# Encoder block, one core: the opening's loads asked for in another order, and the first scale part in two halves

## The reference, cut to what matters

```
mod = silu(c) @ w_ada + b_ada                      # 6 x 2048 columns: shift1, scale1, gate1, shift2, ...
h   = rmsnorm(x, g_mix) * (1 + scale1) + shift1
z   = h @ w_in                                     # latents (832 columns), GQA q, k, v, two branch gates
...                                                # two attentions, output projection, expert-choice FFN
```

## Time and profile before

| | |
|---|---|
| time, median of 3 runs | 2217.11 us (2216.94 to 2217.76) |
| the profiled execution | 2216.92 us, span 2214.6 us, mean granted TensorE clock 0.991 |
| TensorE busy (PE) | 2124.1 us, 96% of the span |
| VectorE busy (DVE) | 871.9 us, 39% |
| ScalarE busy (ACT) | 566.4 us, 26% |
| chain of work that ended last | TensorE 84%, DMA 8%, VectorE 4%, ScalarE 1% |
| DMA | 635.61 MB, 287 GB/s over the span |

### The profile page before, as it was taken

How to read it: one execution, slowest core, us unless ns; L and a number is a source line. 1 busy time by engine, 2 the same in 40 slices (tenths; PEclk the granted TensorE clock), 3 DMA queues, 4 the chain that set the end, 5 groups by cost and what they waited for, 6 DMA issues and landing times.

```text
span 2214.6 us, 26365 instructions
## 1 busy us (share of the span) xinstructions
PE 2124.1 (96%) x10338; PEld 1380.8 (62%) x10338; DVE 871.9 (39%) x1229; ACT 566.4 (26%) x996; POOL 4.7 (0%) x8
## 2 busy tenths in 40 slices
PE   7999999999999999999999899999999999998996
PEld 4777788888887767888888545343534444444432
DVE  4572667666666665445433400202030202121114
ACT  4254442222246664212222511010100000100102
POOL 0000000000000000000000000000000000000000
PEclk9999999999999999999999999999999999999999
DMA  9966775888770100543422699999999999999998
GB/s 335 338 228 248 270 252 169 319 314 288 276 236 26 29 15 1 190 154 130 158 94 76 273 390 425 390 427 427 426 428 429 426 428 426 428 427 426 427 423 309
DMA packets 150319, 635.61 MB, mean 287 GB/s; under 512 B 20418, under 2 KB 33880, under 8 KB 119012
## 3 DMA queue, kind: packets, MB, share of 16 engines
q1 hardware_dynamic: 145636, 626.18, 72.0%
q10 hardware_dynamic: 4608, 8.39, 1.0%
HBM read 621.94 MB, written 12.58 MB: 287 GB/s over the span
## 4 chain that ended last, share of the span: by engine, by line
PE 84%; DMA 8%; DVE 4%; ACT 1%; SPq 1%; issue 1%; DVEq 0%; ACTq 0%
PE bank L1219 25%; PE bank L744 24%; PE bank L746 13%; DMA e_wide<-in_w_e_up 6%; PE bank L1191 5%; PE bank L905 4%; PE bank L794 3%; PE bank L991 2%; PE bank L1211 2%; PE bank L1212 1%; DMA e_slot<-in_w_e_down 1%; PE bank L1201 1%; PE bank L713 1%; PE bank L979 1%; DMA sh_tile<-in_w_ada 1%
## 5 line engine op out<-in xcount | busy, mean ns | idle before, releaser
L1219 PE MATMUL bank<-e_wide,xgT 128*64 128x512 f32 x1456 | 405.5, 603 | 42.8 <-DMA e_slot<-in_w_e_up 16.3
L1398 ACT ACTIVATE w_hi<-stage 128x1024 fp32r<-128x1024 f32 (+1 forms) x168 | 175.3, 1044 | 600.7 <-PE bank L744 339.9
L1801 DVE TENSOR_TENSOR w_lo<-stage,w_hi 128x1024 fp32r<-128x1024 f32 (+1 forms) x168 | 202.4, 1205 | 313.9 <-ACT w_hi L1398 313.2
L1219 PEld LDWEIGHTS bank<-e_wide,xgT 128*64 128x64 f32 x1456 | 129.0, 139 | 292.1 <-issue 289.6
L1219 PE MATMUL bank<-e_slot,xgT 128*64 128x512 f32 x584 | 213.1, 610 | 0.0
L1219 PE MATMUL bank<-e_wide,heT 128*64 128x512 f32 x672 | 168.7, 595 | 0.0
L744 PE MATMUL bank<-hT_hi,w_hi 128*128 128x512 f32 x512 | 159.2, 392 | 0.0
L744 PE MATMUL bank<-hT_lo,w_hi 128*128 128x512 f32 x512 | 158.0, 390 | 0.0
L744 PE MATMUL bank<-hT_hi,w_lo 128*128 128x512 f32 x512 | 157.8, 389 | 0.0
L1872 DVE SCALAR_TENSOR_TENSOR ada_acc<-ada_tile,siluc,ada_acc 128x1024 f32<-128x1024 f32 x116 | 148.7, 1282 | 6.7 <-DMA ada_tile<-in_w_ada 1.2
L2334 DVE TENSOR_TENSOR x<-x,bank 128x512 f32<-128x512 f32 x128 | 79.6, 683 | 175.3 <-PE bank L1212 173.8
(11 more groups left out here) (346 smaller groups left out, 2979.7 us busy)
## 6 DMA issues: line engine op xcount, KB each, us to landing
e_wide<-in_w_e_up SPq DMA_DIRECT2D x49, 2048.0 KB, 16.0
e_wide<-in_w_e_gate SPq DMA_DIRECT2D x42, 2048.0 KB, 13.6
e_wide<-in_w_e_down SPq DMA_DIRECT2D x42, 2048.0 KB, 17.3
ada_tile<-in_w_ada SPq DMA_DIRECT2D x160, 512.0 KB, 5.5
stage<-in_w_in SPq DMA_DIRECT2D x96, 512.0 KB, 6.4
e_slot<-in_w_e_gate SPq DMA_DIRECT2D x43, 1024.0 KB, 15.5
e_slot<-in_w_e_down SPq DMA_DIRECT2D x41, 1024.0 KB, 16.9
e_slot<-in_w_e_up SPq DMA_DIRECT2D x30, 1024.0 KB, 10.6
```

Source lines behind the costliest of these rows:

```text
L1219: last = mm(acc[h][64 * e:64 * e + 64, :], stationary(e), weights(h, e), start=first, stop=end)
L1398: A(w_hi[:, c % NSPLIT, :, 0:width], stage[:, c % NSTAGE, :, 0:width], ACT.Copy).then_inc(hi_ready, 1)
L1801: V.tensor_tensor(w_lo[:, c % NSPLIT, :, 0:width], stage[:, c % NSTAGE, :, 0:width], w_hi[:, c % NSPLIT, :, 0:width].bitcast(F32), ALU.sub ...
```

## The change

In SyncE's queue x is asked for first and the rows after it. The identity and c go by ScalarE's queue, c into a tile of its own (`crow`), which is transposed by itself ahead of everything; the other rows are transposed after tile 1 of x, copied out after tile 2. The first quarter of the scale becomes two parts of 256 columns (`SCALES`), with units of four row blocks by 256 columns (`scale_half`) in banks 6 and 7; the second part is done ahead of chunk 1 and its columns within it. The second quarter's units stand in chunks 2 and 3, its columns within chunk 3. `latent_chunk` waits for `hT_lo` only at its second pass. Shift tiles are loaded later, and the steps are put at other places; `shift_columns(0)` moves from ahead of chunk 14 to ahead of chunk 15. Semaphores and buffer numbers follow.

```diff
@@ load slots
+            if m < 4:
+                return first_scale[:, m, :], once_full[m], 16
             if m < 8:
-                return first_scale[:, m, :], sh_full[m // 2], 32
-            return ada_tile[:, m % NADA, :], ada_full[m % NADA], 16 * ((m - 8) // NADA) + 16
+                return first_scale[:, m, :], x_in[m - 4], 32
+            if 12 <= m < 16:
+                return first_scale[:, m - 8, :], x_in[m - 12], 48
+            return ada_tile[:, m % NADA, :], ada_full[m % NADA], 16 if m < 12 else 16 * ((m - 16) // NADA) + 32
...
@@ SyncE
+            for t in range(T):
+                sp.dma_start(x_sb[:, t, :], x_v[:, t, :]).then_inc(x_in[t], 16)
+            for row, n, src in ((0, 16, g_mix[0]), (16, 16, g_ffn[0]), (32, 4, g_cq[0]), (36, 2, g_ckv[0])):
...
-                    if m >= 8 + NADA:
+                    if m >= 20:
                         sp.wait_ge(sc_used, m - NADA + 1)
-                    k, col = 2 * (m % 8), D + W * (m // 8)
+                    elif m >= 12:
+                        sp.wait_ge(sc_used, m - 8 + 1)
+                    elif 4 <= m < 8:
+                        sp.wait_ge(x_in[m - 4], 16)
+                    ks = 4 if m < 8 else 2
+                    k, col = (4 * (m % 4), D + W // 2 * (m // 4)) if m < 8 else (2 * (m % 8), D + W * (m // 8))
...
-            load_scale(8)
+            load_scale(4)
             load_latent(0)
             load_latent(1)
+            load_scale(6)
+            load_latent(2)
+            load_scale(2)
+            load_latent(3)
+            load_scale(4)
+            load_latent(4)
+            load_latent(5)
...
+            for n, shifts in ((6, (1, 3, 0, 1)), (10, (2, 2, 0, 2))):
+                load_scale(4)
+                load_latent(n)
+                load_shift(shifts[0])
                 load_scale(2)
+                load_latent(n + 1)
+                load_shift(shifts[1])
                 load_scale(2)
+                load_latent(n + 2)
+                load_shift(shifts[2])
+                load_latent(n + 3)
+                load_shift(shifts[3])
             load_latent(14)
-            load_shift(2)
             load_latent(15)
-            load_shift(3)
-            for n, shifts in ((16, 3), (17, 3), (18, 3), (19, 3), (20, 0), (21, 0), (22, 0), (23, 0)):
+            load_shift(5)
+            for n, shifts in ((16, 4), (17, 4), (18, 4), (19, 4), (20, 0), (21, 0), (22, 0), (23, 0)):
@@ TensorE
+            pe.wait_ge(c_in, 32)
+            nc.tensor.transpose(bank[4][:, 0:16], crow[:, :], ident[0:16, 0:16]).then_inc(cols_done, 1)
...
+            def scale_half(h, u):
+                if h == 0 and u == 0:
+                    pe.wait_ge(siluc_ready, 3)
+                tile, full, count = scale_slot(4 * h + u)
+                pe.wait_ge(full, count)
+                for j in range(4):
+                    last = mm(bank[6 + h][32 * j:32 * j + 32, 0:W // 2], sil32[:, 4 * u + j, :], tile[:, j * (W // 2):(j + 1) * (W // 2)],
+                              start=u == 0, stop=u == 3)
+                last.then_inc(sc_used, 1)
...
-                if t == 0:
-                    pe.wait_ge(cols_ready, 4)
-                    for b in (4, 5):
-                        mm(bank[b][:, :], ident[:, :], zeros[:, :], start=True, stop=False)
+                    if t == 3 and i == 1:
+                        scale_half(0, 3)
+                if t == 1:
+                    row_columns()
                 if t == 2:
-                    scale_unit(0, 0)
-            for u in range(1, 4):
-                scale_unit(0, u)
+                    for u in range(3):
+                        scale_half(0, u)
             scale_columns(0)
...
+            def between(n, b):
+                q, u = n // 4, n % 4
+                if (n, b) == (1, 0):
+                    for v in range(4):
+                        scale_half(1, v)
+                elif (n, b) == (1, 2):
+                    scale_columns(1)
+                elif (n, b) in ((2, 0), (2, 2), (2, 3), (3, 0)):
+                    scale_unit(1, ((2, 0), (2, 2), (2, 3), (3, 0)).index((n, b)))
+                elif (n, b) == (3, 2):
+                    scale_columns(2)
+                elif q in (1, 2) and u < 3 and b == 2:
+                    for v in ((0,), (1,), (2, 3))[u]:
+                        scale_unit(q + 1, v)
...
-                if n == 14:
+                if n in (7, 11):
+                    scale_columns(n // 4 + 2)
+                if n == 15:
                     shift_columns(0)
@@ ScalarE
-            act.wait_ge(cols_ready, 2)
-            A(siluc[:, :], pcol[:, 32:48], ACT.Sigmoid).then_inc(sigc_ready, 1)
+            act.dma_start(ident[:, :], consts[:, C_ID:C_FOLD]).then_inc(c_in, 16)
+            act.dma_start(crow[:, :], c[0].rearrange("(k p) -> k p", p=P)).then_inc(c_in, 16)
+            act.wait_ge(cols_done, 1)
+            A(siluc[:, :], bank[4][:, 0:16], ACT.Sigmoid).then_inc(sigc_ready, 1)
...
+            for r, (first, end) in enumerate(((0, 1), (1, 3), (3, 5), (5, 9), (9, 13))):
+                for n in range(first, end):
                     latent_hi(n)
+                scaled_hi(r)
@@ VectorE
             scale_rows(0)
+            scale_part(0)
+            scaled_lo(0)
             latent_lo(0)
-            scale_quarter(0)
             latent_lo(1)
-            scaled_lo(0)
...
+            for r, n, steps in ((2, 4, (0, 0, 1, 2)), (3, 8, (0, 3, 2, 1))):
+                scale_rows(r)
+                latent_lo(n)
+                scale_part(r)
+                scaled_lo(r)
+                shift_steps(steps[0])
+                for i in range(1, 4):
+                    latent_lo(n + i)
+                    shift_steps(steps[i])
+            scale_rows(4)
+            latent_lo(12)
+            scale_part(4)
+            scaled_lo(4)
             shift_steps(2)
+            for n in range(13, 16):
+                latent_lo(n)
+                shift_steps(3)
             ada_finish(0, 0)
```

More of the change, by code:

```diff
@@ L55 @@
 NCOR = 3
-SC_USES = 24 // NADA + 2
+SC_USES = 20 // NADA + 2
 N_Z, N_GATE = 0, 40
@@ L307, in encoder_block @@
         bcol = small("bcol", [P, 96])
-        pcol = small("pcol", [P, 54])
+        pcol = small("pcol", [P, 38])
         siluc = small("siluc", [P, 16])
@@ L325, in encoder_block @@
         limit = small("limit", [32, 2])
-        prow = at("B", 32 * KB, "prow", [54, P])
+        prow = at("B", 32 * KB, "prow", [38, P])
+        crow = at("B", 36 * KB, "crow", [16, P])
         brow = at("B", 32 * KB + 512, "brow", [96, P])
@@ L763, in scale_unit, with scale_columns @@
                 last.then_inc(sc_used, 2)
-            def scale_columns(q):
-                pe.wait_ge(sc_rows_ready, q + 1)
-                for i in range(4):
-                    last = mm(bank[7][:, i:i + 1], sc_rows[:, i * P:(i + 1) * P], ones[:, 0:1], start=True, stop=True)
+            def scale_columns(r):
+                pe.wait_ge(sc_rows_ready, r + 1)
+                for i in range(SCALES[r][1]):
+                    last = mm(bank[7 if r else 6][:, i:i + 1], sc_rows[:, i * P:(i + 1) * P], ones[:, 0:1], start=True, stop=True)
                 last.then_inc(sc_col_done, 1)
@@ L778, in latent_chunk @@
                 for b in range(4):
-                    if b == 2:
-                        between()
+                    between(n, b)
                     if not second:
@@ L1424, in _, with scaled_hi @@
             transposed_x(T - 1)
-            def scaled_hi(q):
-                act.wait_ge(a1_ready, q + 1)
-                if q == 0:
+            def scaled_hi(r):
+                act.wait_ge(a1_ready, r + 1)
+                if r == 0:
                     act.wait_ge(xT_act, 8)
                     act.wait_ge(xT_dve, 8)
-                for k in range(4 * q, 4 * q + 4):
+                for k in range(SCALES[r][0], sum(SCALES[r])):
                     A(hT_hi[:, k, :], xT[:, k, :], ACT.Copy, scale=a1[:, k:k + 1]).then_inc(hT_hi_ready, 1)
@@ L1839, in _ @@
                     transposed_x(t - 1)
+                if t == 2:
+                    columns()
             transposed_x(T - 1)
@@ L1876, in ada_finish, with scale_rows, scale_part, scaled_lo @@
                 V.tensor_tensor(modcol[:, ds(8 * r, 8)], bank[7][:, 0:8], bcol[:, ds(8 * r, 8)], ALU.add).then_inc(ada_col_ready, 1)
[L1878 to L1890 removed]
+            def scale_rows(r):
+                dve.wait_ge(sc_used, 2 * sum(SCALES[r]))
+                width = P * SCALES[r][1]
+                V.tensor_copy(sc_rows[:, 0:width], bank[7 if r else 6][:, 0:width]).then_inc(sc_rows_ready, 1)
+            def scale_part(r):
+                dve.wait_ge(sc_col_done, r + 1)
+                k, n = SCALES[r]
+                link(V.scalar_tensor_tensor(modcol[:, 16 + k:16 + k + n], bank[7 if r else 6][:, 0:n], 1.0, bcol[:, 16 + k:16 + k + n],
+                                            ALU.add, ALU.add))
```

(4 more changed lines are left out.)

131 lines of the change are left out of this document (44 added, 87 removed).

## The result

The changed kernel takes 2221.83 us (median of 13 runs, 2220.03 to 2223.46), the kernel before in the same sessions 2217.11 us (13 runs, 2214.20 to 2218.54): ratio 1.002, 95% interval 1.0013 to 1.0027. That is 4.7 us slower, a little over the 0.2% (4.4 us) from which the prediction calls a kernel slower; the interval reaches to both sides of that line. The profiled executions say the same: 2214.6 us of span before, 2219.3 after, both at a mean granted clock of 0.991. TensorE's busy time is 2122.5 us, where it was 2124.1: nothing was added to its work, it stood idle longer.

What follows compares the result with a forecast made beforehand. TensorE was taken as the bound, unbroken from 153.6 us, with opening and tail deciding when it gets there. Terms -5.8 + 3.05 - 1.2 + 1.9 + 3.0 = +0.95 us gave 2218.0 us, range 2213.8 to 2222.0.

Steps and rivals of the forecast that it cites:

- tail: After the last scale columns: 23 shift steps left on VectorE instead of 19 make the fourth GQA chunk 3.0 us later (1 to 4).
- opening: Up to the first latent chunk: x asked earlier and shorter chains start chunk 0 effectively at 28.6, 5.8 us before 34.4.
- halves and columns: Latent stage: the first scale quarter's second half and its column matmuls now fall among the latents, 3.05 us later (2.5 to 4.4).
- pair of tiles: Second scale quarter, chunk 6: tiles 22 and 23 land behind other loads on SP's queue, 1.9 us later (0 to 2.5).
- scale rows: Latent stage: two waits for copied scale rows go, as fewer shift steps stand ahead on VectorE, 1.2 us earlier.
- behind the fourth chunk: From the fourth GQA chunk TensorE has no pause, so nothing of the tail can be hidden further on.
- A slow clock after the new wait: Tail, after TensorE's new wait: a slow clock would fall where TensorE waits for VectorE 0.8 us later anyway.
- c comes late: Opening rival: c shares the engines with x, lands at 8.2, opening gains only 1.8; sum +4.95, 2222.1 us; chance 0.15.
- Hardly anything: Opening: a whole first scale quarter would land at 23.9, also ahead of the copies, so halving it buys hardly anything.
- 1 KB rows: First scale half's DMA: 341 GB/s, landed 19.2; rival, 1 KB packets cost as 2 KB, +2.25, 2219.3 us; chance 0.10.

Runs made afterwards that it cites:

- e4: The changed kernel with four matmuls of zeros in TensorE's wait ahead of the first GQA chunk; 2221.23 us (ratio 1.002).
- e2: The kernel before, old opening, with the changed kernel's late places of the shift steps, loads and first shift columns; 2222.76 us (ratio 1.0026).
- e3: The changed kernel with c and the identity as first asks on SP's queue, x behind them; 2219.58 us (ratio 1.0013).
- e8: The changed kernel with the ada tile pair 22 and 23 asked for ahead of three shift tiles; 2222.12 us (ratio 1.0025).
- e7: e5 with the first scale quarter whole instead of in two halves; 2215.92 us (ratio 0.9997).
- e11: The kernel before, old opening, with two more shift steps ahead of the last scale columns, two fewer between GQA chunks; 2214.58 us (ratio 0.9983).
- e9: e5 with two more shift steps and their loads ahead of the last scale columns, two fewer between GQA chunks; 2211.15 us (ratio 0.9969).
- e5: The changed kernel with early shift steps (e1) and c with the identity ahead of x on SP's queue (e3); 2213.64 us (ratio 0.9985).
- e10: The changed kernel with ScalarE's four bank copies and hi(16) ahead of the two shifted tiles; 2221.39 us (ratio 1.0019).
- e1: The changed kernel with shift steps, their tile loads and first shift columns early again; 2215.36 us (ratio 0.9992).

## Where the prediction held and where it failed, step by step

The time was 2221.83 us: inside the stated range (2213.8 to 2222.0), at its upper end, and outside the forecast's own (2216 to 2219.5). By the prediction's line of 4.4 us this is "slower", which had 0.14, and not "same", which had 0.81. That the range held is in part luck: its upper end stood for c coming late at its full price, while the tail came out beyond its own bounds (5.8 where 1 to 4 stood). The mechanisms were the ones forecast in the main, but one term, the tail, was mis-sized by 2.8 us.

| term | predicted | measured | from |
|---|---|---|---|
| opening | -5.8 | -4.9 | 34.4 to 29.5, the start the latents go as though begun at |
| halves and columns | +3.05 | +2.7 | lead of 4.9 down to 2.2 at the unit at 59.77 |
| pair of tiles | +1.9 | +2.2 | lead of 2.2 down to 0 at 76.16 |
| scale rows | -1.2 | -1.7 | lead of 0 up to 1.7 at 104.14 |
| tail | +3.0 | +5.8 | 47.7 to 53.5 |
| behind the fourth chunk | 0 | +0.6 | 4.7 of span less 4.05 at the chunk |
| sum | +0.95 | +4.7 | |

- **Tail: the step that failed.** The walk along VectorE's queue had the right order (w_hi late for the first GQA chunk, then w_lo 16, then the fourth chunk), but it ran without waits for tiles. Two came, 0.55 and 1.24 us at 119.87 and 122.40, and modcol stood at +23.8 instead of +21.8 (its end, as in the prediction). The tile of the second wait was asked for at 115.10, when a step had freed a buffer, and took 7.28 us to land. TensorE's wait became 4.79 us instead of 3. Then the clock: "A slow clock after the new wait would fall where TensorE waits for VectorE 0.8 us later anyway" covers only the first 0.85 us. It lasted until 142 us, and the chain goes through these slow matmuls (136.70 for 7.16 us); e4 shows that it cost 0.9 us at the shift columns and 0.7 at the fourth chunk. With the 1.8 us of waits that makes 2.5 to 2.7 of the 2.8 us by which the term was short. Only the clock's part is shown by a run (e4, whose own waits for tiles were 0.4 us longer); the waits' part is argued. No run takes the waits away alone, and in e2, e3 and e8 they are 2.6 to 2.8 us and the tail is only 0.2 to 0.6 us longer, so they need not come through in full. The sum should have priced the tiles: the prediction moved their loads later and counted their traffic for the pair of units, but not for the steps themselves.
- **Opening.** c landed at 6.54 us and not at 4.2, inside the bounds of 3.3 and 8.2. The first square came at 8.51, 1.9 us later than forecast, but the copies to xT ended only 1.2 later (25.7 against 24.5) and the latents effectively 0.9 later, because the squares of tiles 1 to 3 followed at 2.2, 4.2 and 3.2 us where 2.5, 4.1 and 3.6 had been counted. So half of the rival "c comes late" happened and was worth 0.9 us.
- **"Hardly anything" for the halving** was wrong: with c first, e7 puts 2.9 us on it at the first latent and 2.3 us on the median. In the profiled executions 0.35 us of it is left at the fourth chunk.
- **Halves.** 32 half instructions took 1.86 us in the chain, where I took 2.4 and bounded it at 1.85 below: at half the columns they cost half. With 0.34 for the columns that is 2.2 of the 2.7 us; the rest was not placed.
- **Pair and scale rows.** The pair's term was in its bounds, but two errors met in it: the last tile landed at 75.07 where 72.1 was counted, and TensorE came to the pair at 71.63 where 70.2 was. The scale rows gave 0.5 us more than the waits alone: two column blocks that no longer wait also go by in 0.79 us where 1.05 had stood in the chain.
- **1 KB rows.** 341 GB/s was estimated from two rows; 346 was measured from 14 to 16 us. That rival is out. The Trainium skill's page "DMA: Bandwidth & Descriptors", in Specifications, would have line rate for them, and the trace has 346 beside 426 for x: the measurement decides.
- **Behind the fourth chunk.** The first correction matmul comes 4.08 us later than before (186.66 against 182.58). From there to the end it is 2032.6 us, and 2032.0 before; over the profiled executions of all kernels here this stretch is 2031.9 to 2033.0. So the 0.6 us are within what executions differ by, and are not shown to be the change's.

The marks that held: four half units in a row (from 35.2, 0.47 us each where 0.6 stood), a wait of 0.40 us for w_lo inside chunk 0, a wait of 1 to 2 us in chunk 6 (1.05 and 0.31), the last columns at 104. TensorE was idle 4.79 and 0.85 us around the first GQA chunk where "about 5" stood. The first latent matmul (27.3 forecast) came at 28.50. The third and fourth GQA chunk (145.5 and 154.5 forecast) came at 149.12 and 157.61, 3.6 and 3.1 us late, which is most of the error of the sum.

## What to carry to other kernels

Before work is moved later on an engine that is off the critical path, walk its queue to the next place where the critical engine waits for it, with the landing of each tile it needs. Here 4.9 us of lead at the first latent had come down to 1.7 us at the last scale columns, and behind them stood a tail longer by 5.8 us. A lead is worth what the last such place lets through, so the places of the side work are to be set anew with every change ahead of them: with the late places the new opening moved the median by 0.9 us (e2 against the changed kernel, not clear of none), and with c first and early places by about 3.4 (e11 against e9). A small transfer on which a whole chain hangs is asked for ahead of the large ones; in e3 and e5 it stood first on the same queue, and no run tells the order from the queue.

## What the runs showed of the hardware

- The identity (64 KB) and c (8 KB), asked at 0.83 and 1.27 us on ScalarE's queue while 4 MB of x went over SP's, landed 5.2 and 5.3 us after their asks, c at 6.54. The same two as the first asks on SP's queue (c at 0.75, the identity at 1.2 us in e5) were there at 3.06, and the first square of x came 1.3 us earlier (7.20). In Queues, rings and completion order, the page "DMA: Bandwidth & Descriptors" of the Trainium skill has an engine take turns between queues by packets. The trace agrees as far as it goes: the small asks took some 3 us more than as the first asks, and landed before the 8.2 us that two whole asks of x ahead of them would have made; the turns themselves are not in it.
- The granted clock fell to the lower level (0.50, 1.2 of 2.4 GHz) in every kernel with a long pause of TensorE ahead of the first GQA chunk (2.98 to 5.60 us): 0.52 from 134 to 142 in the changed kernel (pause 4.79), 0.60 from 136 to 144 in e2 (5.44), 0.52 from 132 to 134 in e10 (2.98). It did not in e1, where the pause was 1.74 us. It also fell at the fourth chunk in every kernel, behind the thin column matmuls and waits of up to 1.02 us, even in e9, where the wait ahead of the columns is gone (0.66 from 148 to 153 us). With one pause filled with zeros (e4), the fall at the next thin stretch came earlier and was longer.
